# FFN's second product on one Trainium2 core: seven block products in place of eight

## The chip, the cores and the metric

The kernel runs on one core of a Trainium2 chip (trn2). The metric is the device time of one launch in microseconds, as the median of several runs. The profile is one profiled execution. Engines are named as in it: PE is TensorE (PEld its weight loads), DVE is VectorE, ACT is ScalarE, POOL is GpSimd, SP is SyncE, which here issues DMAs.

## The reference, cut to what matters

A transformer layer pair on 1024 tokens of width 1024 (a mixture-of-experts layer, then an attention and state-space layer) ends in a gated FFN, and the end of that FFN is the part that matters here:

```python
FFN_DIM = 2816
...
def rms_norm_2(x, w):
    xf = x.astype(jnp.float32)
    y = xf * lax.rsqrt(jnp.mean(xf * xf, axis=-1, keepdims=True) + NORM_EPS)
    return (y * w.astype(jnp.float32)).astype(x.dtype)
```

In words: the gate half and the up half of the first product go through a causal convolution of three taps, `hidden = silu(gate) * up` has 2816 columns for each of 1024 tokens, and the output is `x + rms_norm_2(hidden @ w_down, norm_ffn_post)`. The product `hidden @ w_down` is 1024 x 2816 by 2816 x 1024 in float32.

## The kernel before, in words

A float32 operand is split in two parts: ScalarE writes a rounded copy, "high" (`split_high`, L125), and VectorE writes the rest, "low" = operand - high (`split_low`, L130). One product of two tiles is then three matmuls into the same PSUM bank: high by high, high by low, low by high (`three_passes`, L135 to L137). Each has 128 x 128 weights (128 tokens of `hidden`, by 128 of the 2816 rows) and 512 moving columns of the weight matrix.

FFN's first product (in `ffn_stage`) is made in 11 turns (`TURNS`), each with a gate half (c = 0) and an up half (c = 1) that use four PSUM banks each; it is itself done in seven block products per pair of tiles, with sums of weight blocks on GpSimd (L4858 to L4864). The 22 rows of `hidden` (`FFN_T = 22`, each 128 x 1024: 128 hidden columns by all tokens) are stored to DRAM two per turn; the last two stay in SBUF. The last turn is written out by hand: `up_turn(TURNS - 1, True)` puts the first splits of the second product between VectorE's `c22_u3` and `c12` (L4824 to L4827), then come `c12`, `c21`, `c11`, the convolutions (L4607), and `hide` (L4614), which makes the last two rows of `hidden`.

`FfnDown` (L4873) is the second product. Its loops go over n, the two halves of 512 output columns, k, the 22 rows of `hidden`, and t, the eight tiles of 128 tokens, one PSUM bank each. For n = 0 a step (one k) needs row k of `hidden` (loaded back from DRAM, split into high and low, kept for n = 1) and one 128 x 512 block of the weights (a ring of three buffers, `down_w`); it gives 8 x 3 = 24 matmuls. For n = 1 only the weights are loaded and split. Between the two halves the eight banks are copied out, even tiles by ScalarE (L5029), odd ones by VectorE (L5052). The last five k of n = 1 (`LAST = 5`) have buffers of their own for their weights, and are multiplied tile by tile, so that a tile's result is ready every 15 matmuls.

Behind each of these tiles the end follows: ScalarE squares and sums it (L5022), VectorE makes the mean (L5068, L5070), ScalarE the root (L5044), VectorE the reciprocal (L5072), two `scalar_tensor_tensor` that scale and add x (L5074, L5076), and VectorE (odd tiles, L5080) or GpSimd (even tiles, L5087) add the second half; SP stores the tile (L4951).

The order is fixed by queues: each engine works through its own list, and waits on counting semaphores. SP issues all loads in one list (`load`, L4927). It loads rows 0 and 1 and three weight blocks when the turn before the last is stored; row 2 (`SOON`) waits for the end of the last combinations, since its place in SBUF is in use till then. On ScalarE and VectorE the first two rows and three weight blocks are split inside the last up turn; all further splits stand behind `hide` on VectorE.

## Time and profile before

| what | us |
|---|---|
| median of 3 runs (2786.56 to 2796.26) | 2788.62 |
| time of the profiled execution | 2786.81 |
| its span, first to last instruction | 2785.1 |
| TensorE busy | 2591.0 |
| VectorE busy | 1858.9 |
| ScalarE busy | 1350.3 |
| GpSimd busy | 547.1 |
| moved by DMA | 439.60 MB |

The page of the profile gives busy time per engine and a row of 40 equal slices of the span (69.6 us each) with busy tenths, and `PEclk`, the TensorE clock granted, in tenths of full speed. A matmul's "busy" time includes its way through the array, and successive ones overlap: how fast they follow each other is read from their start times in the timeline.

### The profile page before, as it was taken

How to read it: one execution, taken by the hardware profiler on the slowest of the kernel's cores; microseconds unless marked ns; L12 is line 12 of the kernel's file. 1: busy time of each engine (PE TensorE's matmuls, PEld its weight loads, DVE VectorE, ACT ScalarE, POOL GpSimd, SP SyncE). 2: the span in 40 equal slices, each digit the busy share in tenths (PEclk: the TensorE clock that was granted, in tenths of full speed). 3: DMA queues.
4: the chain of work that ended last, by engine and by line, in shares of the span. 5: the costliest groups of instructions: out<-in, count | busy, mean ns of one | idle time of the engine just before them, and what ended most of it. 6: DMA issues, size and time to landing. Idle time of an engine off the chain costs nothing. (4 is left out here: it accounts for less than half of the span.)

```text
span 2785.1 us, 39209 instructions
## 1 busy us (share of the span) xinstructions
PE 2591.0 (93%) x14872; PEld 2092.3 (75%) x14873; DVE 1858.9 (67%) x2489; ACT 1350.3 (48%) x2034; POOL 547.1 (20%) x502
## 2 busy tenths in 40 slices
PE   8999978888888699999997899889999899999998
PEld 7988846565677588888885788666787688888887
DVE  5442156676755799999996833777778888886314
ACT  5111056666732577777785432346644333433212
POOL 0000035646510100000001500220001233430000
PEclk9999979898999799999998899999999999999999
DMA  5456221111154599999996411010221232233314
GB/s 191 180 193 259 81 80 50 53 44 54 63 186 179 205 410 411 409 410 409 409 409 233 159 57 45 1 62 1 55 91 53 76 90 69 81 90 117 133 49 163
DMA packets 165714, 439.60 MB, mean 158 GB/s; under 512 B 21916, under 2 KB 102224, under 8 KB 152272
## 3 DMA queue, kind: packets, MB, share of 16 engines
q1 hardware_dynamic: 150976, 383.83, 37.6%
q0 software_dynamic: 8848, 33.03, 3.1%
q10 hardware_dynamic: 5760, 20.97, 1.8%
q8 instruction: 85, 1.39, 0.2%
q14 instruction: 45, 0.37, 0.0%
HBM read 358.63 MB, written 79.17 MB: 157 GB/s over the span
## 5 line engine op out<-in xcount | busy, mean ns | idle before, releaser
L135 PE MATMUL psum<-part,expert_x_high 128*128 128x512 f32 x520 | 207.0, 398 | 2.9 <-issue 1.5
L137 PE MATMUL psum<-part,expert_x_low 128*128 128x512 f32 x520 | 203.2, 391 | 0.0
L135 PE MATMUL psum<-project_w_high,high 128*128 128x448 f32 (+1 forms) x512 | 194.4, 380 | 3.5 <-DVE low L399 3.5
L137 PE MATMUL psum<-project_w_high,low 128*128 128x448 f32 (+1 forms) x512 | 193.5, 378 | 0.0
L136 PE MATMUL psum<-project_w_low,high 128*128 128x448 f32 (+1 forms) x512 | 193.5, 378 | 0.0
L130 DVE TENSOR_TENSOR expert_down_low<-expert_down,expert_down_high 128x2048 fp32r<-128x2048 f32 x62 | 139.3, 2289 | 39.6 <-ACT expert_down_high L125 39.6
L130 DVE TENSOR_TENSOR expert_gate_low<-expert_gate,part 128x2048 fp32r<-128x2048 f32 x64 | 143.9, 2289 | 8.5 <-ACT part L125 7.0
L135 PE MATMUL psum<-part,ffn_w_high 128*128 128x512 f32 x352 | 139.4, 396 | 10.6 <-DVE ffn_u L4576 6.3
L130 DVE TENSOR_TENSOR expert_up_low<-expert_up,part 128x2048 fp32r<-128x2048 f32 x64 | 143.8, 2289 | 1.0 <-ACT part L125 1.0
L136 PE MATMUL psum<-ffn_b_low,ffn_w_high 128*128 128x512 f32 x352 | 138.8, 394 | 0.0
L125 ACT ACTIVATE expert_down_high<-expert_down 128x2048 fp32r<-128x2048 f32 x62 | 115.4, 1909 | 19.4 <-ACT expert_y L2571 19.4
L125 ACT ACTIVATE part<-expert_gate 128x2048 fp32r<-128x2048 f32 x64 | 119.5, 1922 | 6.8 <-DMA h_rows<-out_xs 6.8
L137 PE MATMUL psum<-down_w_high,ffn_hidden_low 128*128 128x512 f32 x312 | 121.4, 389 | 0.0
L125 ACT ACTIVATE part<-expert_up 128x2048 fp32r<-128x2048 f32 x64 | 119.4, 1923 | 0.0
L135 PEld LDWEIGHTS psum<-part,expert_x_high 128*128 128x128 f32 x520 | 98.2, 189 | 24.4 <-issue 1.8
L137 PEld LDWEIGHTS psum<-part,expert_x_low 128*128 128x128 f32 x520 | 97.9, 188 | 22.1
L135 PEld LDWEIGHTS psum<-project_w_high,high 128*128 128x128 f32 x512 | 96.4, 188 | 18.1 <-DVE low L399 4.7
L125 ACT ACTIVATE ffn_w_high<-ffn_w 128x1024 fp32r<-128x1024 f32 x44 | 44.4, 1051 | 133.5 <-POOL ffn_sums L4864 133.5
L4858 POOL TENSOR_TENSOR ffn_sums<-ffn_w 128x512 f32<-128x512 f32 x19 | 38.4, 2019 | 359.8 <-DMA ffn_w<-in_ffn_w_up_dram 359.8
L137 PEld LDWEIGHTS psum<-project_w_high,low 128*128 128x128 f32 x512 | 96.4, 188 | 13.8
L136 PEld LDWEIGHTS psum<-project_w_low,high 128*128 128x128 f32 x512 | 96.5, 188 | 13.7
L135 PE MATMUL psum<-ffn_t_high,ffn_w_high 128*128 128x512 f32 x264 | 103.2, 391 | 0.8 <-DVE ffn_t_low L130 0.7
(756 smaller groups left out, 7259.5 us busy)
## 6 DMA issues: line engine op xcount, KB each, us to landing
expert_gate<-in_w_gate_dram SPq DMA_DIRECT2D x32, 2048.0 KB, 10.2
expert_up<-in_w_up_dram SPq DMA_DIRECT2D x32, 2048.0 KB, 10.1
expert_down<-in_w_down_dram SPq DMA_DIRECT2D x32, 2048.0 KB, 10.8
ffn_w<-in_ffn_w_up_dram SPq DMA_DIRECT2D x44, 512.0 KB, 4.3
y_rows<-expert_y ACTq DMA_DIRECT2D x32, 512.0 KB, 10.7
hidden_rows<-ffn_hidden SPq DMA_DIRECT2D x20, 512.0 KB, 3.1
ffn_hidden<-hidden_rows SPq DMA_DIRECT2D x20, 512.0 KB, 3.8
down_w<-in_ffn_w_down_dram SPq DMA_DIRECT2D x39, 256.0 KB, 2.6
```

The source lines that it names most:

```text
L125: return act.activation(high, x, ACT.Copy)
L130: return v.tensor_tensor(low, x, high, ALU.subtract)
L135: pe.matmul(out, left[0], right[0], start=start, stop=False)
L136: pe.matmul(out, left[0], right[1], start=False, stop=False)
L137: return pe.matmul(out, left[1], right[0], start=False, stop=stop)
L4858: pool.tensor_tensor(s1, a21, a22, ALU.add).then_inc(summed[c], 1)
```

## The change

The product is cut into 2 x 2 blocks: tokens 0 to 511 and 512 to 1023, rows 0 to 10 and 11 to 21 of `hidden` and of the weights, output columns 0 to 511 and 512 to 1023. With A the blocks of hidden (A11 the first tokens, first rows; A21 the second tokens, first rows) and B those of the weights, seven products are made, in this order (1 and 7 step about):

- 1: A11 by B11. 7: (A11 - A21) by (B22 - B12). 6: (A22 - (A11 - A21)) by (B11 + B22 - B12). 5: (sum of 6's left with A11) by (B12 - B11). 4: A22 by (6's right - B21). 3: (A12 - 6's left) by B22. 2: A12 by B21.

A product has 11 steps (k), a step 4 tiles of 128 tokens with three matmuls each. The left operands' sums are made by VectorE in place in the rows of `hidden` (`sum_of`, 44 instructions of 128 x 512), the right operands' by GpSimd (`turn_weights`, 44 of 128 x 512), from blocks that SP loads into four buffers (`SOURCES`). Each of the 77 steps has its own splits, left and right, of 128 x 512, into a ring of six. Results leave the banks by eight copies on ScalarE and 20 additions and subtractions on VectorE, and one addition per tile on GpSimd. The norm of the second tokens is done during products 3 and 2, on ScalarE and GpSimd; that of the first tokens at the end.

```diff
-    RING = 3
-    AHEAD = 2
+    HALF = FFN_T // 2
+    PRODUCTS = (1, 7, 6, 5, 4, 3, 2)
+    STEPS = len(PRODUCTS) * HALF
+    QUARTER = TT // 2
+    RING, SOURCES = 6, 4
+    EARLY = 2
     LAST = 5
...
+    SUMS, TURNED = (7, 6, 5, 3), (7, 6, 5, 4)
+    LOADED = {1: (0, 0), 3: (1, 1), 2: (1, 0)}
+    PARTS = {7: ((1, 1), (0, 1)), 6: ((0, 0),), 5: ((0, 1), (0, 0)), 4: ((1, 0),)}
+    EVICT_AT = 4
...
     def load(self, sp, room_left):
...
+        load_hidden(0)
+        for n, (m, k) in self.steps():
+            if n == 1:
+                load_hidden(1)
+            if n == self.EARLY:
+                room_left("slots")
+            if m in self.LOADED:
+                if n >= self.RING:
+                    sp.wait_ge(self.used, n - self.RING + 1)
+                sp.dma_start(self.right[n % self.RING], block(self.LOADED[m], k)).then_inc(self.loaded[n % self.RING], 16)
+            if m == 1 and 0 < k < HALF - 1:
+                load_hidden(k + 1)
+            if m == 7 and k >= 4:
+                for row in range(HALF + 2 * (k - 4), min(HALF + 2 * (k - 3), FFN_T - 2)):
+                    load_hidden(row)
+            for i, part in enumerate(self.PARTS.get(m, ())):
+                s = self.source_no(m, k) + i
+                if s >= self.SOURCES:
+                    sp.wait_ge(self.turned_ready, self.done_with(s - self.SOURCES))
+                sp.dma_start(self.source[s % self.SOURCES], block(part, k)).then_inc(self.source_loaded[s % self.SOURCES], 16)
...
     def multiply(self, pe, bank_left):
...
+        for n, (m, k) in self.steps()[0:self.STEPS - self.LAST]:
+            pe.wait_ge(self.left_low_ready, n + 1)
+            pe.wait_ge(self.right_low_ready, n + 1)
+            for t in range(self.QUARTER):
+                if k == 0:
+                    wait_bank(m, t)
+                last = multiply_tile(n, m, k, t)
...
+        pe.wait_ge(self.left_low_ready, self.STEPS)
+        pe.wait_ge(self.right_low_ready, self.STEPS)
+        for t in range(self.QUARTER):
+            for n, (m, k) in self.steps(self.STEPS - self.LAST):
+                last = multiply_tile(n, m, k, t)
...
+    def low(self, v, n, m, k):
+
+        i = n % self.RING
+        if n + 1 < self.STEPS:
+            self.sum_of(v, n + 1, *self.steps()[n + 1][1])
+        v.wait_ge(self.left_high_ready, n + 1)
+        split_low(v, self.left_low[i], self.left_of(m, k), self.left_high[i]).then_inc(self.left_low_ready, 1)
+        v.wait_ge(self.right_high_ready, n + 1)
+        split_low(v, self.right_low[i], self.right_of(n, m, k), self.right_high[i]).then_inc(self.right_low_ready, 1)
...
+    def turn_weights(self, pool):
...
+                elif m == 5:
+                    n = self.step(5, k)
+                    pool.wait_ge(self.used, n - self.RING + 1)
+                    ins = pool.tensor_tensor(self.right[n % self.RING], sources[0], sources[1], ALU.subtract)
...
+                t = k - self.EVICT_AT
+                if m == 5 and 0 <= t - 1 < self.QUARTER:
+                    self.add_third_row(pool, t - 1)
```

The end of the first tokens, per tile (VectorE; ScalarE squares and takes the root between):

```diff
+        for t in range(self.QUARTER):
...
+            v.wait_ge(self.ended, t + 1)
+            v.tensor_tensor(c11[:, t, :], c11[:, t, :], bank[self.banks(2) + t][:], ALU.add).then_inc(self.first_made, 1)
+            v.wait_ge(self.first_made, t + 1)
+            v.tensor_tensor(self.turned[t], c11[:, t, :], self.gain[0], ALU.mult).then_inc(self.first_gained, 1)
+            v.wait_ge(self.squared, 3 * self.QUARTER + t + 1)
...
+            for h, of in enumerate((self.turned[t], c12[:, t, :])):
+                last = v.scalar_tensor_tensor(out=x[:, h, :], in0=of, scalar=first[:, 3, now], in1=x[:, h, :], op0=ALU.mult, op1=ALU.add)
```

In the last up turn, ScalarE and VectorE now split the first two steps (`EARLY = 2`), where before they split two rows and three weight blocks:

```diff
                 if last:
-                    down.take_low(v, 0)
-                    down.take_low(v, 1)
-                    down.weights_low(v, 0, 2)
+                    for n, (m, k) in down.steps()[0:down.EARLY]:
+                        down.low(v, n, m, k)
```

## Rows read from the trace of the kernel before

**Rows 1.** The page: busy time by engine, and the clock granted in 40 slices.
```profile
PE 2591.0 (93%) x14872; PEld 2092.3 (75%) x14873; DVE 1858.9 (67%) x2489; ACT 1350.3 (48%) x2034; POOL 547.1 (20%) x502
...
PEclk9999979898999799999998899999999999999999
```

**Rows 2.** Busy time in stretches: the second product.
```profile
core 0: us, PE busy (x) PEld busy (x) DVE busy (x) ACT busy (x) POOL busy (x), PEclk, DMA share, GB/s
...
2537.60:2777.10 239.50, 239.50 (x1057) 198.08 (x1055) 81.54 (x111) 61.52 (x104) 6.09 (x4) 1.00 0.34 118
```

**Rows 3.** Timeline of PE: start, duration, what, at the product's start and end.
```profile
2537.38 0.39 PE L137 MATMUL psum<-part,ffn_w_low 128*128 128x512 f32 x1
2537.61 0.39 PE L135 MATMUL psum<-down_w_high,down_early 128*128 128x512 f32 x1
...
2776.74 0.39 PE L137 MATMUL psum<-ffn_hidden_low 128*128 128x512 f32 x1
```

**Rows 4.** Groups by line and shape in the second product, ACT and DVE.
```profile
L125 ACT ACTIVATE down_w_high<-down_w 128x512 fp32r<-128x512 f32 x36 | 22.5, 624 | 84.4 <-DMA down_w<-in_ffn_w_down_dram 84.4
L5022 ACT ACTIVATE ffn_hidden<-down_y 128x512 f32<-128x512 f32 x8 | 5.0, 630 | 0.2
...
L130 DVE TENSOR_TENSOR down_w_low<-down_w,down_w_high 128x512 fp32r<-128x512 f32 x36 | 24.8, 689 | 81.8 <-ACT down_w_high L125 81.7
```

**Rows 5.** Timeline of DVE around the start of the second product.
```profile
2533.72 1.29 DVE L130 TENSOR_TENSOR down_w_low<-down_w,down_w_high 128x512 fp32r<-128x512 f32 x2
...
2537.81 0.69 DVE L4597 TENSOR_TENSOR ffn_u<-ffn_u,psum 128x512 f32<-128x512 f32 x1 [1.60 <-PE psum L137]
...
2543.44 2.35 DVE L4614 TENSOR_TENSOR ffn_hidden<-ffn_acc,ffn_hidden 128x1024 f32<-128x1024 f32 x2
2545.71 1.22 DVE L130 TENSOR_TENSOR ffn_hidden_low<-ffn_hidden,down_early 128x1024 fp32r<-128x1024 f32 x1
```

**Rows 6.** DMA issues of the second product: count, size, median us to landing.
```profile
ffn_hidden<-hidden_rows SPq DMA_DIRECT2D x18, 512.0 KB, 3.8
down_w<-in_ffn_w_down_dram SPq DMA_DIRECT2D x36, 256.0 KB, 2.6
...
ffn_hidden<-in_ffn_w_down_dram SPq DMA_DIRECT2D x5, 256.0 KB, 5.2
```

**Rows 7.** Timeline and stretches of PE behind two idle times in the first product.
```profile
2175.04 0.80 PE L135 MATMUL psum<-part,ffn_w_high 128*128 128x512 f32 x1 [4.28 <-DVE x L4576]
...
2180.76 0.44 PE L136 MATMUL psum<-ffn_t_low,ffn_w_high 128*128 128x512 f32 x1
...
2203.41 0.79 PE L135 MATMUL psum<-part,ffn_w_high 128*128 128x512 f32 x1 [6.30 <-DVE ffn_u L4576]
...
2175.00:2181.00 6.00, 5.96 (x14) 4.69 (x15) 5.91 (x7) 2.32 (x2) 0.00 (x0) 0.51 0.40 158
```

**Rows 8.** Timelines of DVE and of POOL where both work, in the first product.
```profile
2339.85 0.68 DVE L4583 TENSOR_TENSOR ffn_mid<-ffn_mid,psum 128x512 f32<-128x512 f32 x1
...
2348.38 1.28 DVE L4607 SCALAR_TENSOR_TENSOR ffn_hidden<-x,ffn_taps,ffn_hidden 128x1023 f32<-128x1023 f32 x1 [0.28 <-ACT ffn_hidden L4337]
2349.81 6.54 DVE L4607 SCALAR_TENSOR_TENSOR ffn_hidden<-x,ffn_taps,ffn_hidden 128x1022 f32<-128x1022 f32 x3 [0.15 <-DVE ffn_hidden L4607]
...
2339.06 1.29 POOL L4864 TENSOR_TENSOR ffn_sums<-ffn_w,ffn_sums 128x512 f32<-128x512 f32 x1
...
2353.00 2.27 POOL L4862 TENSOR_TENSOR ffn_w<-ffn_w 128x512 f32<-128x512 f32 x1
```

**Rows 9.** Timelines of ACT and DVE behind the last matmul.
```profile
2777.17 0.60 ACT L5022 ACTIVATE ffn_hidden<-psum 128x512 f32<-128x512 f32 x1 [2.09 <-PE psum L137]
...
2777.89 0.16 DVE L5068 TENSOR_TENSOR down_mean<-down_square 128x1 f32<-128x1 f32 x1 [1.17 <-ACT ffn_hidden L5022]
...
2778.50 0.17 DVE L5072 RECIPROCAL down_rstd<-down_root 128x1 f32<-128x1 f32 x1 [0.27 <-ACT down_root L5044]
2778.70 0.75 DVE L5074 SCALAR_TENSOR_TENSOR ffn_hidden<-psum,down_rstd,ffn_b 128x512 f32<-128x512 f32 x1
...
2780.03 0.68 DVE L5080 TENSOR_TENSOR feat<-feat,ffn_hidden 128x512 f32<-128x512 f32 x1
```

More of the change, by code:

```diff
@@ L4480, in _ @@
             act.wait_ge(made1[1], TURNS * 2)
-            for k in range(2, FFN_T):
-                if k == FFN_T - 2:
-                    act.wait_ge(hidden_ready, TURNS * 2)
-                down.take_high(act, k, k > 2)
-            down.square(act)
+            down.highs(act)
         @block.vector
@@ L4824, in up_turn @@
                 if last:
-                    down.take_low(v, 0)
-                    down.take_low(v, 1)
-                    down.weights_low(v, 0, 2)
+                    for n, (m, k) in down.steps()[0:down.EARLY]:
+                        down.low(v, n, m, k)
                 else:
@@ L4843, in _ @@
             hide(TURNS - 1)
-            for k in range(2, FFN_T):
-                if k == FFN_T - 2:
-                    v.wait_ge(hidden_ready, TURNS * 2)
-                down.take_low(v, k, k > 2)
-            down.norm(v)
+            down.lows(v)
         @block.gpsimd
@@ new lines, in step, with steps, sum_no, turned_no @@
+    def step(self, m, k):
+        i = self.PRODUCTS.index(m)
+        return 2 * k + i if i < 2 else i * self.HALF + k
+    def steps(self, first=0):
+        order = [(m, k) for k in range(self.HALF) for m in self.PRODUCTS[0:2]] + [(m, k) for m in self.PRODUCTS[2:] for k in range(self.HALF)]
+        return list(enumerate(order))[first:]
+    def sum_no(self, m, k):
+        return self.SUMS.index(m) * self.HALF + k
+    def turned_no(self, m, k):
+        return self.TURNED.index(m) * self.HALF + k
@@ new lines, in source_no, with load_no, banks, left_of @@
+    def source_no(self, m, k):
+        before = sum(len(self.PARTS[i]) for i in self.TURNED[0:self.TURNED.index(m)]) * self.HALF
+        return before + len(self.PARTS[m]) * k
+    def load_no(self, n):
+        return sum(i % self.RING == n % self.RING and m in self.LOADED for i, (m, k) in self.steps() if i <= n)
+    def banks(self, m):
+        return 4 * (self.PRODUCTS.index(m) % 2)
+    def left_of(self, m, k):
+        row = k + (self.HALF if m in (4, 2) else 0)
+        n = 1 if m in (7, 6, 3, 4) else 0
+        return self.hidden[:, row, n * BANK:(n + 1) * BANK]
@@ new lines, in right_of, with highs, square @@
+    def right_of(self, n, m, k):
+        return self.turned[k] if m in (7, 6, 4) else self.right[n % self.RING]
+    def highs(self, act):
+        c11, c12, c21, c22 = self.c11, self.c12, self.c21, self.c22
+        second, first = self.stats
+        def square(of, t, to):
+            done = self.squares_done
+            if done:
+                act.wait_ge(self.squared, done)
+            act.activation(self.junk[done % 2], of[:, t, :], ACT.Square, accum_out=to[:, t:t + 1]).then_inc(self.squared, 1)
+            self.squares_done += 1
+        self.squares_done = 0
+        for n, (m, k) in self.steps(self.EARLY):
+            self.high(act, n, m, k)
+            if (m, k) == (6, self.COPIES_AT):
+                for of, to in ((1, c11), (7, c21)):
+                    for t in range(self.QUARTER):
+                        self.wait_made(act, of, t)
+                        act.activation(to[:, t, :], self.bank[self.banks(of) + t][:], ACT.Copy).then_inc(self.copied, 1)
+            if (m, k) == (3, self.FOURTH_AT + self.QUARTER):
+                for t in range(self.QUARTER):
+                    act.wait_ge(self.fifth_added, 2 * t + 1)
+                    square(c22, t, second[:, 1, :])
+                for t in range(self.QUARTER):
+                    act.wait_ge(self.fourth_added, t + 1)
+                    square(c21, t, second[:, 0, :])
+            if (m, k) == (3, self.SCALES_AT):
+                act.wait_ge(self.mean_ready, 1)
+                act.activation(second[:, 3, :], second[:, 2, :], ACT.Sqrt).then_inc(self.root_ready, 1)
+            if (m, k) == (3, self.HALF - 1):
+                for t in range(self.QUARTER):
+                    act.wait_ge(self.scaled, 1)
+                    for of in (c21, c22):
+                        last = act.activation(of[:, t, :], of[:, t, :], ACT.Copy, scale=second[:, 3, t:t + 1])
+                    last.then_inc(self.second_gained, 1)
+        for t in range(self.QUARTER):
+            act.wait_ge(self.third_added, t + 1)
+            square(c12, t, first[:, 1, :])
+        for t in range(self.QUARTER):
+            act.wait_ge(self.first_made, t + 1)
+            square(c11, t, first[:, 0, :])
+            act.wait_ge(self.mean_ready, t + 2)
+            act.activation(first[:, 3, t:t + 1], first[:, 2, t:t + 1], ACT.Sqrt).then_inc(self.root_ready, 1)
```

403 lines of the change are left out of this document (223 added, 180 removed).

## The prediction, made before the changed kernel was run

> **What bounds the kernel now.** I read the page first: TensorE is busy 93% of the span, and its clock is near full in the last slices [rows 1]. Then the stretch of the second product: in its 239.5 us TensorE is busy all the time at granted clock 1.00 (2.4 GHz), VectorE 81.5, ScalarE 61.5, GpSimd 6.1 us [rows 2]. Last the timeline of PE: the first matmul starts at 2537.61, the last at 2776.74, and the code has 2 x 22 x 8 x 3 = 1056 of them. So 239.13 us over 1055 gaps is 0.2267 us each, without a hole [rows 3]. This stage is bound by the number of matmuls. What counts besides is what happens where the stage begins, and the 8 us behind its last matmul.
>
> **What is removed.** The new product has 7 x 11 x 4 x 3 = 924 matmuls of the same shape: 132 fewer, 132 x 0.2267 = **29.9 us** off the path, if TensorE never waits. A step is now 12 matmuls, 2.72 us, where it was 24.
>
> **The start.** Before, 48 matmuls (two rows of hidden) were ready in advance: 10.9 us from 2537.61, to 2548.5, and the third row's low part was ready at 2545.71 + 1.22 = 2546.9 [rows 3, 5]. Now two steps are ready: 24 matmuls, 5.44 us, until 2543.05. The third step's splits stand on VectorE behind the convolutions and `hide`, which end at 2545.71 [rows 5]; then come the sum for the next step, the left low and the right low. Two 128x512 of that kind took 1.29 us, one 0.69, so they follow each other at 0.60 [rows 4, 5]: 0.60 + 0.60 + 0.69 = 1.9, ready at 2547.6, TensorE back at 2547.7. That is 4.7 us of waiting. ScalarE's part is no later: its high parts need the weight block, issued when the last matmul of the first product is done (2537.8), landed some 3 us later [rows 3, 6].
>
> GpSimd, idle here before, now works at this very time: its sources for the second and third sum are issued behind two other loads at about 2539 and 2541 and land 3 us later [rows 6], while VectorE runs the convolutions and `hide`. The rows show what this does. A GpSimd `tensor_tensor` of 128x512 takes 1.29 us beside a VectorE instruction that reads PSUM, which itself keeps its 0.68; but beside VectorE's instructions with both inputs in SBUF it takes 2.27, and these take 6.54 / 3 = 2.18 where one alone takes 1.28 [rows 8]. So a collision costs VectorE 0.9 us. Two of them here: 1.8. **Waiting at the start: 4.7 + 1.8 = 6.5 us**; bounds 4.7 (none) and 7.4 (three).
>
> Behind such a pause the clock falls. After 4.28 us idle, 14 matmuls started within 5.72 us, where 13 gaps at 0.2267 are 2.95; the granted clock of that stretch is 0.51, which is 1.2 GHz [rows 7]. The pause of 6.30 us was followed by about ten at that pace as well. **Clock: 2.5 us** (bounds 0 and 2.8).
>
> **The middle.** TensorE needs a step each 2.72 us. ScalarE: two high parts at about 0.52 to 0.62, 1.2 us [rows 4]; eight copies, eight squares and eight scalings in three places, the longest 8 x 0.82 = 6.6 us, against a ring that lets it be five steps (13.6 us) ahead. VectorE: two lows, in 44 of the 77 steps a sum, and 20 results in and out of PSUM: in product 5, 3 x 0.60 + 4 x 0.60 / 11 = 2.0 us a step. To this come GpSimd's collisions, in product 5 15 instructions in 11 steps: 15 x 0.9 / 11 = 1.2. The sum, 3.2 to 3.3, is over 2.72 by some 0.6, so 11 steps lose 6 to 7 us. Product 6 is just even (1.8 + 0.9 = 2.7), product 4 has no sums (1.2 + 0.44 + 0.9), product 3 hardly a GpSimd instruction. The lead that can be lost: a step's slot is free five steps ahead, 13.6 us, less the chain of GpSimd's sum, ACT's high and VectorE's low (2.3 + 0.6 + 0.7, some 3.3 with waits overlapped), 10.3 us. So it holds and I cost the middle at **0**; if the lead is gone, each further microsecond is TensorE's.
>
> What the Trainium skill says here speaks against this change: "SBUF — State Buffer", section "Summary: rules for kernel authors", has it that of a GpSimd instruction and a VectorE instruction with two SBUF inputs the second to issue blocks fully until the first is done. The direction is what the rows show, but not quite the size: the whole of GpSimd's 1.29 us would give 15 x 1.29 = 19.4 us in product 5, and 41.6 us of VectorE's time against 29.9 of TensorE's, 11.7 over; by this the forecast would be 1.4 us later.
>
> Transfers: in product 7 a pair of steps (5.44 us) needs three weight blocks and one row of hidden, 1.3 MB, and for k = 4 to 7 two more rows, 2.3 MB: 430 GB/s. The stretch before moved 118 GB/s with the DMA engines busy a third of the time, so about 350 is full [rows 2]; four pairs fall behind by some 5 us, which SP's lead of five steps holds. A block took 2.6 us to land, 5.2 with four others in flight [rows 6].
>
> **Before the last five steps.** TensorE now waits for all 77 splits. The last block's slot is free, and its load issued, only when step 71 of 77 is done; one more step (2.72 us) is left. Load 0.3 + 2.6, high 0.62, low 0.69 and three handovers are 4.6 us [rows 4, 6]: **1.9 us** of waiting (0 to 3). Before, the last five had buffers of their own.
>
> **The end.** Before, behind the last matmul (2777.13) came square, mean, root, reciprocal, two scalings and a sum to 2780.71: 3.6 us [rows 9]. Now VectorE adds the result to c11 first (0.69), the square follows (0.63 + 0.19), the mean and root 0.6, the reciprocal, two scalings (0.67 + 0.75), one sum less: 3.9 us behind a tile. Without the hand-over at the end VectorE's period is 3.75 us a tile, and a tile comes each 15 x 0.2267 = 3.40: 0.35 more for each of three tiles. Together 3.9 + 1.05 - 3.6 = **1.3 us** (0 to 2). The second tokens' norm on GpSimd, 16 instructions at up to 2.27 = 36 us, starts near step 62, 41 us before the end, so it is hidden, barely; if not, it is the tail that grows.
>
> **The sum.** Against the profiled execution (2786.8, of which 1.7 lies outside the span): -29.9 + 6.5 + 2.5 + 0 + 1.9 + 1.3 = -17.7 gives 2769.1. The median of the runs shown is 1.8 above that execution, so the forecast is 2788.6 - 17.7 = **2770.9**.
>
> **The rivals.**
> A, the gain comes almost whole: no collisions at the start, the clock stays, the loads are in time. -29.9 + 4.7 to 6 gives 2763 to 2765. For it: the collisions come about only if GpSimd's loads land before 2547; against it: both pauses of over 4 us in the first product were followed by 1.2 GHz [rows 7]. And 4.7 us follow from the order on VectorE alone.
> B, GpSimd's chain binds in product 5. Its four source buffers hold two sums: sum (2.27), two issues (0.9), landing (5.2 when the queue is full) is 8.5 us for two steps, 4.3 a step against 2.72, or 17 us over 11 steps [rows 6, 8]; less the lead of 10.3 that is 7 us, and one or two clock falls, 2.5 each. 2770.9 + 11 = 2782. For it: nothing here shows two engines fed so closely; against it: at 2.6 us a landing it is 5.9 for two, 0.2 a step too much.
> C, slower than before. Place: products 6 to 4. Where TensorE waits a little in each step, its clock stays at 1.2 GHz, and a step takes 12 x 0.427 = 5.1 us instead of 2.72 (pace from [rows 7]), 2.4 more. It decides from about 11 such steps on (26 us more than forecast); for 22 steps it gives 2770.9 + 53 = 2824. Against it: at that pace TensorE is busy without a gap, VectorE and GpSimd catch up, and in rows 7 the clock was back after 5.7 us.
> D, fewer matmuls but no gain that can be measured, from several of the above: 2782 to 2790. That the matmuls are not fewer is excluded by the loop bounds.
>
> **How the numbers follow.** What a measurement of this kernel can tell from no change is about 0.3%, 8.4 us. Forecast 0.60, A 0.16, B 0.14, C 0.06, D 0.04. The likeliest case gives 2770.9. The range takes A's lower side with the end unchanged (2760) and B with two clock falls (2784). Faster means under 2780.2: forecast, A, and a good third of B: 0.82. Same: the rest of B, and D: 0.12. Slower: 0.06.
>
> **What would show it.** In the profile after: 924 matmuls in some 221 us; one idle time of PE of 6 to 7 us near 2543, ended by VectorE's low part, and 0.43 us between matmuls behind it; a wait near 2 us before the last 60 matmuls; GpSimd's sums at 2.2 rather than 1.3 us. Idle time of PE in product 5, ended by a right low part behind a GpSimd sum, would speak for B; one ended by a left low or a sum for VectorE as the bound. The forecast is wrong if the first pause is absent, or if waits in the middle sum to more than 5 us.

## The result, and the profile after

The changed kernel takes **2793.02 us** (median of 20 runs, 2789.13 to 2801.56); the kernel before, run beside it, 2787.89 (20 runs, 2783.74 to 2796.26). The ratio is 1.0017, 95% interval 1.001 to 1.0025: slower by some 5 us, within the 0.3% that the prediction called the same. The forecast was 2770.9, its range 2760 to 2784. The time lies outside it.

The profiled execution has a span of 2793.0 us. The page of the profile after, against [rows 1]:

```profile
PE 2573.9 (92%) x14740; PEld 2073.9 (74%) x14741; DVE 1984.4 (71%) x2627; ACT 1396.3 (50%) x2131; POOL 644.5 (23%) x562
...
PEclk9999979898999799999998999999999999999999
```

There are 132 matmuls fewer, and VectorE is busy 125.5 us longer. Next the timeline of PE in the second product after, first and last matmul and each idle time ahead of one (start, duration, what, in brackets the idle time and what ended it); it answers to [rows 3]:

```profile
2538.90 0.39 PE L135 MATMUL psum<-down_right_high,down_left_high 128*128 128x512 f32 x1
...
2550.10 0.76 PE L135 MATMUL psum<-down_right_high,down_left_high 128*128 128x512 f32 x1 [5.60 <-DVE down_right_low L130]
...
2602.41 0.47 PE L135 MATMUL psum<-down_right_high,down_left_high 128*128 128x512 f32 x1 [1.14 <-DVE down_right_low L130]
2607.47 0.47 PE L135 MATMUL psum<-down_right_high,down_left_high 128*128 128x512 f32 x1 [2.08 <-DVE down_right_low L130]
2618.80 0.77 PE L135 MATMUL psum<-part,down_left_high 128*128 128x512 f32 x1 [7.11 <-ACT down_c L5112]
...
2684.53 0.47 PE L135 MATMUL psum<-down_right_high,down_left_high 128*128 128x512 f32 x1 [0.44 <-DVE down_right_low L130]
...
2758.82 0.47 PE L135 MATMUL psum<-part,down_left_high 128*128 128x512 f32 x1 [0.40 <-DVE part L130]
2767.14 0.77 PE L135 MATMUL psum<-down_right_high,down_left_high 128*128 128x512 f32 x1 [5.34 <-DVE part L130]
...
2783.25 0.39 PE L137 MATMUL psum<-part,down_left_low 128*128 128x512 f32 x1
```

From first to last it is 244.35 us, where it was 239.13. The 923 gaps at 0.2267 are 209.2, so some 35 us are lost, where none was. Summing what each gap has over 0.2267 gives 34.8, by place (steps count from 0, 12 matmuls each; "clock" is matmuls at 0.43 us behind a pause; the granted clock of 2552 to 2555 is 0.50, 1.2 GHz):

| place | lost, us | forecast |
|---|---|---|
| start, before step 2: wait 5.6, clock 2.0 | 7.8 | 9.0 |
| before steps 20, 21 and 22, the border of products 7 and 6: waits 1.1, 2.1, 7.1, and clock | 14.1 | 0 |
| product 4, four waits of 0.4, each with some 0.2 behind it | 2.7 | 0 |
| product 2, three such waits | 2.0 | 0 |
| before the last five steps: wait 5.3, clock 2.7 | 8.3 | 1.9 |

Behind the last matmul the span runs 9.75 us on, where it was 8.36: 1.4 (forecast 1.3). The product also begins 1.3 us later than in the profile before (2538.90, 2537.61); between profiles of kernels that are the same up to there this moves by more (2538.01 in e1_copies, 2546.22 in e2_paced), so it is no effect of the change. Together 5.2 + 1.4 + 1.3 = 7.9, the difference of the two spans; the medians differ by 5.1.

What stands behind the waits is seen in the timelines of POOL and DVE around steps 20 to 22, against [rows 8]. POOL (a row with x9 holds nine instructions that follow each other without a gap):

```profile
2584.32 1.29 POOL L5247 TENSOR_TENSOR feat<-down_source 128x512 f32<-128x512 f32 x1 [4.58 <-DMA down_source<-in_ffn_w_down_dram]
...
2596.49 3.53 POOL L5250 TENSOR_TENSOR down_turned<-down_turned,down_source 128x512 f32<-128x512 f32 x2 [0.49 <-DMA down_source<-in_ffn_w_down_dram]
2599.99 15.18 POOL L5250 TENSOR_TENSOR feat<-feat,down_source 128x512 f32<-128x512 f32 x9
```

DVE, at the same time:

```profile
2597.08 1.78 DVE L5146 TENSOR_TENSOR ffn_hidden<-ffn_hidden 128x512 f32<-128x512 f32 x1
...
2602.18 1.76 DVE L5153 TENSOR_TENSOR ffn_hidden<-ffn_hidden 128x512 f32<-128x512 f32 x1
2603.87 1.78 DVE L130 TENSOR_TENSOR down_left_low<-ffn_hidden,down_left_high 128x512 fp32r<-128x512 f32 x1
2605.57 1.75 DVE L130 TENSOR_TENSOR down_right_low<-feat,down_right_high 128x512 fp32r<-128x512 f32 x1
2607.24 1.77 DVE L5153 TENSOR_TENSOR ffn_hidden<-ffn_hidden 128x512 f32<-128x512 f32 x1
...
2615.65 0.68 DVE L130 TENSOR_TENSOR part<-down_turned,part 128x512 fp32r<-128x512 f32 x1
```

GpSimd makes product 6's eleven sums in a row, one each 1.70 us, and in just this time eleven instructions of VectorE in a row take 1.7 to 1.8 in place of 0.68. They alternate, one for one: each GpSimd sum costs VectorE 1.70 - 0.60 = **1.1 us**. A step of VectorE (one sum, two lows) is 5.06 us here (2602.18 to 2607.24), against 2.72 of TensorE's. And the lead, the time from a step's last split to its first matmul, is small already: step 8's was 7.3 us, and step 19's last split ends at 2597.16, 1.2 us before its first matmul at 2598.38. In product 7 GpSimd waited for its sources (4.58 in the row above), and VectorE in turn stood still five times, 17.1 us in all, for the high parts of such sums.

The longest wait names ScalarE. Its timeline there:

```profile
2614.14 0.63 ACT L125 ACTIVATE down_left_high<-ffn_hidden 128x512 fp32r<-128x512 f32 x1 [3.88 <-DVE ffn_hidden L5153]
...
2618.08 3.98 ACT L5112 ACTIVATE down_c<-psum 128x512 f32<-128x512 f32 x8
```

TensorE wants the bank of product 1 for product 6, and the copy of it stands in ScalarE's list behind the splits of product 6's fourth step (`COPIES_AT = 3`). These wait for VectorE's sums, which are late. With VectorE on time this place in the list costs nothing (e5_vsum below has it, and no wait there); with the lead gone it is 7.1 us late.

At the end the same pattern, in the timelines of DVE and ACT ahead of the last 60 matmuls:

```profile
2738.22 1.74 DVE L130 TENSOR_TENSOR down_left_low<-ffn_hidden,down_left_high 128x512 fp32r<-128x512 f32 x1 [5.61 <-ACT down_left_high L125]
...
2753.49 1.78 DVE L130 TENSOR_TENSOR part<-feat,part 128x512 fp32r<-128x512 f32 x1
2755.19 0.68 DVE L5206 TENSOR_TENSOR down_c<-down_c,psum 128x512 f32<-128x512 f32 x1
...
2766.31 0.68 DVE L130 TENSOR_TENSOR part<-feat,part 128x512 fp32r<-128x512 f32 x1
...
2732.65 5.02 ACT L5127 ACTIVATE down_c<-down_c,down_stats 128x512 f32<-128x512 f32 x8 [1.28 <-DVE down_stats L5213]
```

VectorE stands still for 5.6 us while ScalarE scales, then works from 2738.2 to 2767.0 without a hole, eleven instructions of it at 1.7 to 1.8 beside GpSimd's norm (16 instructions, 2734.11 to 2759.8). The addition that reads PSUM keeps its 0.68.

**The theory**: the matmuls saved are given back because GpSimd's help costs VectorE more than the work taken from it, in bursts, at two places where TensorE has no lead left. **The rivals**: the chain of transfers (late sources in product 7, the last blocks' loads at the end), and the order on ScalarE.

### The profile page after: what moved, and what is told of

Read it like the earlier page. It is cut to its first block and busy times, and to the rows that moved or that the text cites. A ratio compares the mean times of both kernels' runs of the same rounds, so it can differ in the third digit from the quotient of the medians.

```text
span 2793.0 us, 39523 instructions
## 1 busy us (share of the span) xinstructions
PE 2573.9 (92%) x14740; PEld 2073.9 (74%) x14741; DVE 1984.4 (71%) x2627; ACT 1396.3 (50%) x2131; POOL 644.5 (23%) x562
## 5 line engine op out<-in xcount | busy, mean ns | idle before, releaser
L135 PE MATMUL psum<-part,ffn_w_high 128*128 128x512 f32 x352 | 139.4, 396 | 10.6 <-DVE ffn_u L4574 6.3
L2676 POOL COPY expert_pick<-ids 128x1 int32 x30 | 14.4, 481 | 454.9 <-PE psum L2479 454.9
```

The lines of the kernel that those rows point to most:

```text
L135: pe.matmul(out, left[0], right[0], start=start, stop=False)
L2676: pool.tensor_copy(pick[u][:], ids[:, at]).then_inc(picked[u], 1)
```

## The experiments

Each stands against the kernel before, run beside it on the same chip; "lost" is TensorE's sum over 0.2267 in the run's profile (the changed kernel: 34.8). Medians are of 5 to 11 runs of a kernel, and single times of one kernel differ by up to 15 us, in part before the second product begins (at 2549.13 in e14_front_end's profile, at 2539.08 in e15_all's). So small effects are read from "lost", and from the ratio, beside 1.0017 of the changed kernel.

| run | median, us | before | ratio (95%) | lost |
|---|---|---|---|---|
| e1_copies | 2788.86 | 2788.5 | 1.0005 (0.9995 to 1.0014) | 28.2 |
| e2_paced | 2787.89 | 2788.5 | 1.0003 (0.9993 to 1.0012) | 28.7 |
| e3_fill | 2776.33 | 2788.5 | 0.9965 (0.9951 to 0.9979) | 17.3 |
| e4_norm | 2785.99 | 2788.5 | 0.9991 (0.9982 to 1.0001) | 25.1 |
| e5_vsum | 2778.0 | 2788.01 | 0.9965 (0.9953 to 0.9978) | 17.1 |
| e6_vnorm | 2793.0 | 2788.01 | 1.0022 (1.0011 to 1.0032) | 30.8 |
| e7_start | 2789.67 | 2788.01 | 1.0004 (0.9994 to 1.0014) | 30.3 |
| e8_prefetch | 2794.33 | 2788.01 | 1.0026 (1.0014 to 1.0039) | 33.5 |
| e9_spread | 2791.18 | 2788.27 | 1.0004 (0.9994 to 1.0015) | 31.4 |
| e10_front | 2775.19 | 2788.27 | 0.9946 (0.9932 to 0.9959) | 14.4 |
| e11_both | 2773.12 | 2788.27 | 0.9947 (0.9933 to 0.996) | 13.3 |
| e12_all | 2775.76 | 2788.27 | 0.9958 (0.9944 to 0.9971) | 13.3 |
| e13_end | 2785.79 | 2787.6 | 0.9989 (0.998 to 0.9998) | 24.8 |
| e14_front_end | 2767.64 | 2787.6 | 0.9918 (0.9903 to 0.9934) | 6.4 |
| e15_all | 2764.94 | 2787.6 | 0.9917 (0.9903 to 0.9931) | 4.5 |

**e1_copies**: the copies two steps earlier in ScalarE's list.

```diff
-    COPIES_AT = 3
+    COPIES_AT = 1
```

> The eight copies of products 1 and 7 stand two steps earlier in ScalarE's list (behind the splits of the second step of product 6, not the fourth). Nothing else differs. Theory P (place in the queue): the 7.1 us in which TensorE waited for the first copy came about because ScalarE could not reach it before VectorE had made two more sums; the wait shrinks to under 1.5 us, and with the half-speed stretch behind it the time falls by 6 to 8 us against the changed kernel. Rival V (VectorE binds): TensorE then waits the same microseconds for low parts in the next steps; the wait only moves, and the time falls by under 3 us.

The 7.1 us are gone from PE's waits, and in their place stand three others on VectorE's lows, 1.42, 2.02 and 1.06, and one of 1.17 in product 5. Of 35 us lost, 6.6 are back, and by the ratios 3 to 4 us of time, between what the two theories gave. So the order on ScalarE is not the cause by itself, but it made a late VectorE dearer.

**e2_paced**: GpSimd makes the sums of products 6 and 4 no earlier than the ring lets their step begin.

```diff
                     pool.wait_ge(self.right_low_ready, self.step(7, k) + 1)
+                    pool.wait_ge(self.used, self.step(6, k) - self.RING + 1)
...
                     pool.wait_ge(self.right_low_ready, self.step(6, k) + 1)
+                    pool.wait_ge(self.used, self.step(4, k) - self.RING + 1)
```

> GpSimd's sums for products 6 and 4 each wait until the ring has come within six steps of them, so that GpSimd makes one sum per step and no longer ten in a row. Theory B (bursts): what hurts is that VectorE loses 1.1 us on every instruction while ten sums run one behind the other; spread out, the waits of 3.2 and 7.1 us in product 6 and of four times 0.4 us in product 4 go, 10 us or more off the time. Rival S (the sum counts): each of the 44 sums costs VectorE 1.1 us wherever it stands, and product 5, where they were spread before, is followed by a later start of the others; the time moves by less than 3 us. Third: in product 6 the sums come too late, since a sum then has to wait for its turn, and the time grows.

The waits of 1.1 and 2.1 fall to 0.4 and nothing, the one for the copies stays at 5.1, and a wait of 0.8 comes in product 5: 6.1 us back, and about 4 by the ratios, less than theory B and more than rival S gave. Spread over time the same collisions cost less, but no fewer of them come.

**e3_fill** takes the collisions away and leaves the queue: GpSimd fills each of the 44 blocks with a constant instead of summing its sources, with the same waits. It leaves the sums of the weight blocks out.

```diff
-                    ins = pool.tensor_tensor(self.turned[k], sources[0], sources[1], ALU.subtract)
+                    ins = pool.memset(self.turned[k], 0.5)
```

> GpSimd's 44 sums of weight blocks are left out: it fills the same 128x512 blocks with a constant instead, with the same waits, so it writes SBUF at the same points but reads none. All loads stay. Theory R (shared reads): VectorE's instructions with two SBUF inputs fall back from 1.78 to 0.68 us beside them; the waits in product 6 (3.2 and 7.1 us) shrink to under 3 us together, those in product 4 go, the start pause is 4.5 instead of 5.6 us; the time falls by 12 to 18 us. Rival T (transfers): the lead is lost in product 7 where loads come late (GpSimd waited up to 12 us for its sources); then the waits of product 6 stay over 6 us though VectorE is fast. If writing alone disturbs VectorE as well, its instructions stay over 1 us.

All waits before product 2 are gone but the start's (4.5), also the one that rival T had the late loads cause. Timelines of POOL and DVE in that run:

```profile
2599.82 0.53 POOL L5250 MEMSET feat<- 128x512 f32 x1 [0.20 <-DMA down_source<-in_ffn_w_down_dram]
...
2599.99 0.68 DVE L5153 TENSOR_TENSOR ffn_hidden<-ffn_hidden 128x512 f32<-128x512 f32 x1
```

A GpSimd instruction that only writes SBUF leaves VectorE's at 0.68. So the loads, which are all still there, do not bind on their own before product 2; what binds is GpSimd reading SBUF beside VectorE. The Trainium skill ("SBUF — State Buffer", "Who interferes with whom") says of a VectorE instruction with two SBUF inputs that it contends with a GpSimd instruction that reads SBUF and not with one that only writes it; both halves agree with these rows, 1.78 and 0.68.

**e4_norm**: the 16 instructions of GpSimd's norm cut to 16 columns (the rest of the second tokens' norm is left out).

> GpSimd's 16 instructions for the norm of the second 512 tokens take 16 of 512 columns each (the rest of these products and sums is left out). Theory N: TensorE's last wait (5.3 us before the last 60 matmuls) and three waits of 0.4 us before it come from VectorE's backlog, 16 collisions at 1.1 us; the last wait falls to the 2 us that the chain of load and splits of the last step gives, the time by 4 to 8 us. Rival L: the last wait is the load's chain alone (ScalarE waited 1.9 us for each of the last blocks); it stays over 4 us and the time within 2 us.

The small waits in product 2 are gone, and the last wait is 1.6 instead of 5.3, without matmuls at 0.43 behind it. PE and ACT there:

```profile
2761.72 0.47 PE L135 MATMUL psum<-down_right_high,down_left_high 128*128 128x512 f32 x1 [1.64 <-DVE part L130]
...
2760.22 0.63 ACT L125 ACTIVATE part<-feat 128x512 fp32r<-128x512 f32 x1 [1.95 <-DMA feat<-in_ffn_w_down_dram]
```

Now ScalarE waits for the load of the last block: this is the chain that the prediction priced at 1.9.

**e5_vsum**: all the work kept, the 44 weight sums made by VectorE itself, each one step ahead in its own list.

```diff
+            ins = v.tensor_tensor(self.turned[k], sources[0], sources[1], ALU.subtract)
...
+        if n + 1 < self.STEPS and n != self.EARLY - 1:
+            self.turn_next(v, n + 1)
```

> The 44 sums of weight blocks are made by VectorE itself, each behind the low parts of the step before; GpSimd keeps its four additions in product 5 and the norm of the second tokens. Theory R (a GpSimd sum costs VectorE 1.1 us of waiting, one of its own costs 0.6): VectorE has less to do in products 7 to 4 than now, 44 x 0.5 = 22 us less, and the waits of TensorE in products 6 and 4 go; the time falls by 8 to 15 us against the changed kernel. Rival Q (queue): VectorE now stands still whenever a source block is late, and splits behind it wait; GpSimd waited up to 12 us for sources in product 7, so new waits of TensorE come in product 7, and the time stays within 4 us or grows.

VectorE has 44 instructions more to do, and TensorE waits less. The waits of PE in this run's second product (in total, times, longest):

```profile
PE psum L135 <- DVE part L130: 6.2, 3, 5.3
PE psum L135 <- DVE down_right_low L130: 5.0, 2, 4.5
```

Only the start (4.5), the end (5.3) and three small ones of product 2 are left. It is as fast as e3_fill, which makes no sums at all. The start is 4.54, where the prediction had 4.7 without collisions.

**e6_vnorm**: the norm of the second tokens on VectorE, a multiply and an addition in each of product 2's first eight steps. **e8_prefetch**: product 2's weight blocks loaded early into the `turned` buffers, free behind product 4.

```diff
+            if m == 2 and k < 2 * self.QUARTER:
...
+                v.tensor_tensor(of[:, u, :], of[:, u, :], self.gain[h], ALU.mult).then_inc(self.gained, 1)
...
+                added = v.tensor_tensor(xs[:, h, :], xs[:, h, :], of[:, u, :], ALU.add)
```

```diff
+                if m == 2:
+                    sp.wait_ge(self.right_low_ready, self.step(4, k) + 1)
+                    sp.dma_start(self.turned[k], block(self.LOADED[m], k)).then_inc(self.hidden_loaded[k], 16)
```

> The norm of the second tokens (16 multiplications and additions of 128x512) moves from GpSimd to VectorE, two in each of the first eight steps of product 2. Theory R: VectorE saves 16 x (1.1 - 0.6) = 8 us of its time there and the wait before the last 60 matmuls falls from 5.3 to some 2 us, as it did when these instructions were cut to 16 columns (1.6); the time falls by 4 to 7 us. Rival: VectorE, which must then wait in order for ScalarE's eight scalings, gives low parts later, and the wait stays over 4 us.

> The 11 weight blocks of product 2 are loaded into the buffers of the turned blocks, free since product 4, and no longer into the ring whose slot is free only five steps before. Theory L: the wait before the last 60 matmuls (5.3 us) has the load of the last block in its chain; it falls by 2 to 3 us, to about 3, the time by 2 to 4. Rival N (VectorE's backlog behind GpSimd's norm decides alone): the wait stays at 5 us, the time within 1.5 us.

Neither moved the last wait: 5.13 and 5.31, as their rivals had it. In e6_vnorm the collisions are gone, but ScalarE's eight scalings still stop VectorE for 5.6 us, and then its steps take 2.53 us, and 3.1 in the four with an addition, about TensorE's 2.72: it catches nothing up. In e8_prefetch the load is no longer late, but VectorE is.

**e7_start**: three steps ready before the first product ends, with the buffers of one ring place and two others placed elsewhere.

```diff
-    EARLY = 2
+    EARLY = 3
```

> A third step (A11 by B11, second row) is split inside the last up turn, into buffers that are free by then. Theory S: the pause at the start (5.6 us) is what VectorE's list makes of a lead of two steps; with three steps it is 2.72 + 1.2 shorter, 1 to 2 us, and too short for the fall of the clock; the time falls by 5 to 7 us. Rival: the loads for the next steps, which SP issues only when the first product is done, are late next, and the pause is over 3 us with the clock falling as before; under 3 us gained.

Its PE rows, start and product 6:

```profile
2548.47 0.66 PE L135 MATMUL psum<-down_right_high,down_left_high 128*128 128x512 f32 x1 [2.52 <-DVE down_right_low L130]
...
2612.50 0.76 PE L135 MATMUL psum<-part,down_left_high 128*128 128x512 f32 x1 [8.33 <-ACT down_c L5112]
```

The start wait fell by 3.1 us. The clock fell behind it all the same (1.7 us), against what I expected, so the start loses 4.3 us in place of 7.8. The 8.33 at the copies, in place of 7.11, is no price of the early step: e8_prefetch, e9_spread and e13_end, whose edits all lie behind this place, show 8.38, 8.33 and 8.33 too, and the waits at the border sum to 10.2 us here and 10.3 in the changed kernel. VectorE is as late there as it was.

**e9_spread**: ScalarE's scalings two to a step over four steps, the reciprocal two steps earlier. **e10_front**: e5, e1 and e7 together. **e11_both**: e10_front with the spread scalings. **e12_all**: that with the early loads.

```diff
+            t = n - self.step(3, 9)
+            if 0 <= t < self.QUARTER:
+                act.wait_ge(self.scaled, 1)
+                for of in (c21, c22):
+                    last = act.activation(of[:, t, :], of[:, t, :], ACT.Copy, scale=second[:, 3, t:t + 1])
```

> The changed kernel with one thing moved: the root and the reciprocal of the second tokens come in step 8 of product 3 (before: reciprocal in step 10), and ScalarE's eight scalings, 5.0 us in a row in step 10, are spread two to a step over steps 9 and 10 of product 3 and 0 and 1 of product 2. Theory: the wait of 5.3 us before the last 60 matmuls (and the 2.7 us at half clock behind it) is a backlog of VectorE, which loses 5.6 us while ScalarE scales and then works without a hole beside GpSimd's norm, each step a little longer than TensorE's. So with the hole gone and GpSimd's norm some 6 us earlier, the last wait falls to under 2 us without a clock fall: 5 us less than the changed kernel, 2788 beside 2788 before, ratio 1.000. Rival 1, the chain of the last loads: the wait stays at 5.3 and the ratio at 1.0017. Rival 2, GpSimd's norm simply costs VectorE 16 x 1.1 us wherever it stands: the wait shrinks by no more than 1 us.

> Three edits together, which were tried one by one before: all 44 sums of weight blocks on VectorE, ScalarE's eight copies two steps earlier in product 6, and three steps instead of two ready before the first product ends. Theory: with GpSimd off the sums VectorE has the lead to take up what the third early step moved into product 6 when it was tried alone, so the start pause falls from 4.5 to 2.5 us with nothing in its place, and the clock behind it loses 1.7 instead of 2.1: 2.4 us under the 2778.0 of sums on VectorE alone, that is 2775.6 beside 2788.0, ratio 0.9955. Rival: the third early step comes back in product 6 as it did alone (8.3 us in place of 7.1), ratio 0.9965 or above.

> The kernel of the three front edits (sums on VectorE, copies two steps earlier, three early steps) with the scalings spread as in the run before that. Theory of a VectorE backlog at the end: it loses the last wait of 5.3 us and most of its 2.7 us at half clock, 6 us less than the three front edits alone: 2769.6 beside 2788.0, ratio 0.9934. By the rival of the load chain it equals the kernel of the three front edits, 0.9955.

> As the kernel with front edits and spread scalings, and product 2's weight blocks loaded early into buffers that are free behind product 4, so that the last load hangs on no slot of the ring. Alone this changed nothing. Theory: once the backlog of VectorE is gone, what is left before the last 60 matmuls is the load chain that the prediction priced at 1.9 us (1.64 us measured where GpSimd's norm was cut short); it goes here: 1.6 us less than the kernel before it in this list, 2768 beside 2788.0, ratio 0.9928. Rival: GpSimd's norm still holds VectorE back, and the two kernels are equal, with the same wait in both.

e10_front did as expected: start wait 2.7, and no other wait before product 2. (Its rival rests on the 8.3 us of e7_start, which the early step had not caused.) But the last wait stayed in all four (5.6, 5.3, 5.7, 5.3): spreading the scalings and loading early are not enough, and what I expected of e9_spread, e11_both and e12_all failed. Rival 2 of e9_spread stands. (In e9_spread's profile the start's wait is 6.7 us, though nothing was changed there; of its 31.4 lost some 1.7 are due to that.) Timelines of POOL, DVE and PE in e12_all, where the load and the scalings are out of the way:

```profile
2737.42 1.62 POOL L5285 TENSOR_TENSOR ffn_hidden<-ffn_hidden,down_c 128x512 f32<-128x512 f32 x1
...
2729.32 1.77 DVE L130 TENSOR_TENSOR down_right_low<-feat,down_right_high 128x512 fp32r<-128x512 f32 x1
2731.01 1.78 DVE L130 TENSOR_TENSOR down_left_low<-ffn_hidden,down_left_high 128x512 fp32r<-128x512 f32 x1
...
2745.52 0.68 DVE L130 TENSOR_TENSOR part<-feat,part 128x512 fp32r<-128x512 f32 x1
...
2746.35 0.77 PE L135 MATMUL psum<-down_right_high,down_left_high 128*128 128x512 f32 x1 [5.33 <-DVE part L130]
```

While GpSimd works, a step of VectorE is 2 x 1.70 = 3.40 us, 0.68 more than TensorE's. GpSimd ends at 2739.0, and VectorE then goes at full pace (0.60 an instruction) to its last split without a hole, and is 5.3 us late. The last 60 matmuls begin only when the splits of all 77 steps are done, five steps ahead of use, which is the whole lead that the ring allows. In the changed kernel step 71's splits end at 2758.67, just before their use, and the last ones at 2766.99: 8.3 us of VectorE's work against one step of TensorE's. So the wait is 5.31 to 5.35 us in all nine runs, the changed kernel among them, whose lead is gone by step 71; a step before, the same lack of lead costs 0.4 us. Even with a lead of 3.9 us at step 71 e6_vnorm, which had the norm's work left to do on VectorE, waited 5.1.

**e13_end** therefore takes GpSimd out and makes room: scalings spread, the norm on VectorE over the eight steps from step 9 of product 3, and the four additions of product 3 behind the last split, where VectorE idles. What the additions alone are worth (4 x 0.6 us) isn't separated from the rest; e4_norm had them in their old place and a last wait of 1.6. **e14_front_end** is e10_front with this, **e15_all** that with the early loads.

```diff
-            if now and m == 2:
-                v.wait_ge(self.fifth_added, 2 * t + 2)
...
+            j = n - self.step(3, 9)
+            if 0 <= j < 2 * self.QUARTER:
...
+        for t in range(self.QUARTER):
+            v.wait_ge(self.fifth_added, 2 * t + 2)
```

> The changed kernel with its end rearranged: scalings spread as in e9_spread; the second tokens' norm made by VectorE (one multiply and one add per step, 1.2 us, over the eight steps from step 9 of product 3), so that GpSimd has nothing to do there; and the four additions of product 3's result (0.6 us each) placed behind VectorE's last split instead of in steps 4 to 7 of product 2. Theory 1, a backlog of VectorE: GpSimd's norm and VectorE's splits go in lock step at 3.40 us a step of two splits, against 2.72 of TensorE's, and TensorE needs VectorE's full lead of five steps before the last 60 matmuls. With 1.2 + 1.2 = 2.4 us a step VectorE keeps its lead; the last wait becomes that of the load chain, 1.6 to 1.9 us, with no clock fall: about 6 us under the changed kernel's 2793, 2787, ratio 0.9995 to 1.000. Theory 2, something else ends the wait (ScalarE's work, a transfer): it stays at 5.3 us and the ratio at 1.0017.

> The three front edits (sums of weight blocks on VectorE, copies two steps earlier, three early steps) together with the rearranged end. GpSimd is then idle in the whole second product. Theory 1: of the 13.3 us that the front edits with spread scalings still lost, 6 go (5.6 us of waiting before the last matmuls becomes 1.6 to 1.9, and its 2.4 us at half clock go): 2767 beside 2788, ratio 0.9925. Theory 2: no better than the front edits alone, 0.9946.

> As e14_front_end, and product 2's weight blocks loaded early into buffers that are free behind product 4. Theory 1: what is left before the last 60 matmuls is only the load chain, and it goes: 1.6 to 1.9 us less than e14_front_end, 2765.5, ratio 0.992, TensorE's only wait of over 1 us left is the one at the start (2.7 us). Theory 2: equal to e14_front_end. As a third possibility it gives back about 1 us, since ScalarE waited 3.1 us for the first of these blocks when this was tried with GpSimd's norm.

All three came out by theory 1. The last wait of PE in e13_end, and the load that it hangs on, in ACT's timeline:

```profile
2759.95 0.47 PE L135 MATMUL psum<-down_right_high,down_left_high 128*128 128x512 f32 x1 [1.47 <-DVE part L130]
...
2758.45 0.63 ACT L125 ACTIVATE part<-feat 128x512 fp32r<-128x512 f32 x1 [1.57 <-DMA feat<-in_ffn_w_down_dram]
```

In e14_front_end it is 1.60, and in e15_all, with the block loaded early, it is gone. All of PE's waits in e15_all's second product, and that product as one stretch (us, then busy time and number of PE, PEld, DVE, ACT and POOL, granted clock, DMA share, GB/s):

```profile
PE psum L135 <- DVE down_right_low L130: 2.7, 1, 2.7
...
2539.00:2753.00 214.00, 211.30 (x926) 174.33 (x924) 187.76 (x303) 111.77 (x201) 8.54 (x4) 0.99 0.56 197
```

That is 213.79 us from the first matmul to the last, 25.3 less than before, with GpSimd making four instructions. **e15_all beats both kernels**: 2764.94, ratio 0.9917. Its medians beside e14_front_end's differ by 2.7 us, the ratios hardly; that the early loads gain their 1.6 us is shown by the traces, not by the times.

## Why the prediction was wrong, point by point

- **132 matmuls fewer, 29.9 us: right.** 924 came, and in e15_all they take 209.2 us and 4.5 of waiting.
- **The start, 6.5 + 2.5: right in kind.** 5.60 and 2.0. One of the two collisions came about (the sum at 2547.00 took 1.75 instead of 0.68), and without GpSimd's sums the wait is 4.54 (e5_vsum), against 4.7 from VectorE's order alone.
- **The middle, 0: this step failed.** It lost 18.8 us (14.1, 2.7 and 2.0 in the table); its waits alone are 13.2, where more than 5 was to be the sign of a wrong forecast. The price of a collision was not far off: 1.1 where I took 0.9. What was wrong is how they were counted. I spread them over a product, one to a step of product 6 ("just even") and of product 4. But GpSimd isn't paced by TensorE: it waits only for its sources and for the block's last use, and when these are there it makes eleven sums in 19 us. So VectorE has three collisions in a step of product 6 (5.06 us) and two in one of product 4 (3.40), against TensorE's 2.72. And the burst in product 6 met a lead of 1.2 us, not of 10.3.

  That lead went in product 7, by the transfers that I had held "by SP's lead". VectorE's longest stop there, and two stretches (columns as in [rows 2]; the last three numbers are the granted clock, the DMA engines' busy share and GB/s):

```profile
2568.59 0.69 DVE L130 TENSOR_TENSOR down_right_low<-feat,down_right_high 128x512 fp32r<-128x512 f32 x1 [6.83 <-ACT down_right_high L125]
...
2552.00:2556.00 4.00, 4.00 (x15) 3.19 (x14) 4.00 (x6) 2.19 (x4) 1.80 (x1) 0.72 0.00 1
2560.00:2585.00 25.00, 25.00 (x112) 20.69 (x111) 11.07 (x18) 7.55 (x13) 4.55 (x4) 1.00 1.02 385
```

  For 4 us nothing was moved: SP's next load, step 8's, waits for step 2 to be done (`used`, `RING`), and step 2 stood behind the start's pause. Then the DMA engines are full, and at 385 GB/s the 2.3 MB of a pair of steps take 6.0 us against TensorE's 5.44. So 350 was somewhat low as a full rate, and what the sum lacked is that the start's pause stops the loads too.

  Late sources alone cost nothing in the middle: e3_fill and e5_vsum have them, leads of 2.8 and 3.4 us at step 15, and no wait. Collisions that are spread out cost less (e2_paced). That bursts would be harmless with all sources in time isn't shown; no run has that.
- **Product 5, the lead given away.** I costed it at 6 to 7 of the 10.3 us of lead. It took all: step 33's last split was ready 10.6 us before its first matmul, step 43's 0.2 us. Timelines of DVE and PE:

```profile
2639.27 0.69 DVE L130 TENSOR_TENSOR down_right_low<-down_right_raw,down_right_high 128x512 fp32r<-128x512 f32 x1
2675.81 1.78 DVE L130 TENSOR_TENSOR down_right_low<-down_right_raw,down_right_high 128x512 fp32r<-128x512 f32 x1
...
2650.55 0.39 PE L135 MATMUL psum<-down_right_high,down_left_high 128*128 128x512 f32 x1
2677.75 0.46 PE L135 MATMUL psum<-down_right_high,down_left_high 128*128 128x512 f32 x1
```

  So there was no wait in product 5 itself, but by little: in e1_copies one of 1.17 us came, in e2_paced one of 0.82. The four waits of product 4 are what followed, its burst meeting no lead. Here are the stretches from product 6 on:

```profile
2598.70:2640.00 41.30, 30.97 (x122) 24.31 (x121) 36.79 (x43) 18.89 (x35) 17.76 (x11) 0.88 0.24 74
2640.00:2670.00 30.00, 30.00 (x134) 24.85 (x133) 29.85 (x28) 10.63 (x17) 20.42 (x13) 1.00 0.47 155
```

  In the first VectorE is busy 36.8 of 41.3 us, in the second 29.85 of 30.
- **ScalarE's copies were costed as work only.** I held work of 6.6 us at most (the copies took 4.0) against a ring of five steps, and not what is queued ahead of them: they stand behind splits that wait for VectorE. TensorE's waits at this border are 10.3 us, and 4.5 with the copies two steps earlier (e1_copies).
- **Before the last five steps, 1.9: right for what it names, wrong in which wait comes last; the second step that failed.** The load chain is 1.5 to 1.6 us (e4_norm, e13_end, e14_front_end) and goes with early loads. But GpSimd's norm was costed only as a transfer of work that must be hidden (36 us in 41), and at nothing for VectorE. It made the wait 5.3, and the clock fell behind it: 8.3 in place of 1.9.
- **The end, 1.3: right**, 1.4.
- **The rivals.** None held. B had GpSimd's chain bind in product 5, where TensorE didn't wait and the ring, not the sources, paced GpSimd. C had the clock stay at 1.2 GHz from product 6 on: behind each pause the matmuls went at 0.43 for 13 at most, and then at 0.2267, also in the steps of product 4 with a wait of 0.4 each, so the time stood far under 2824. D, no gain that can be measured from several causes together, is nearest, but was given 0.04 and ended at 2790, below the 2793.0 measured. The causes were not independent: without GpSimd's sums the waits in products 6 and 4 are gone (e3_fill, e5_vsum), and without those of the norm 3.7 us of the last wait (e4_norm).

I weighed the Trainium skill's rule ("SBUF — State Buffer", "Summary: rules for kernel authors": the second to issue blocks fully) as a matter of price, 1.29 or 0.9. The rows give 1.1, in between. By either price the middle would still have been 1.4 us at most in my sum; what it lacked is when GpSimd's instructions come.

## What to carry to other kernels

Before work is moved from VectorE to GpSimd, compare what VectorE gets rid of (0.60 us for a 128x512 sum here) with what each of GpSimd's instructions takes from it (1.1 us when it reads SBUF beside a VectorE instruction with two SBUF inputs): where VectorE is the one that others wait for, the help cost more than the work, and making the 44 sums on VectorE was 15 us faster. The Trainium skill ("Perfetto Trace Analysis", "Optimizing Scalar/DVE Operations") says that moving operations between these two might not help, because of the shared port; here it did harm (e5_vsum against the changed kernel). Count collisions by when the helper runs, not by an average, and look for points where the consumer needs the producer's whole lead, such as a change of loop order at the end: what is late there is never caught up. And where there is no wait, look at how much lead is left: product 5 showed none and had used all of it.

## What the runs showed of the hardware that was not expected

- GpSimd and VectorE go in strict turns: GpSimd's 128x512 addition goes from 1.29 to 1.70 us a piece, VectorE's from 0.60 to 1.70, for eleven in a row. VectorE's instructions with one input in PSUM stay at 0.68 beside the same GpSimd instructions, and so do those with two SBUF inputs beside a fill by GpSimd.
- Behind waits of 2.5 us and more, TensorE started 5 to 13 matmuls at about 0.43 us (1.2 GHz), which cost 1.5 to 3.0 us each time, with no relation to the wait's length (2.7 us: 1.7; 8.3 us: 2.5, 1.6). Behind waits of 1.0 to 1.9 us there was none; behind four of 2.02 to 2.08 us, none once (e1_copies) and five to seven three times (the changed kernel, e4_norm, e6_vnorm), from four to six matmuls later on.
